# Low weights of feature pieces in the other half of a 256-byte stretch, and high and low products in turn

## What is computed

```
proj = rmsnorm(h) @ w_in                     # q, k, v, u, y of the first block
q = rmsnorm(h) @ w_cq; k, v = mem @ w_ck, mem @ w_cv
hid = square(relu(rmsnorm(h) @ w_mlp_in)); h = h + hid @ w_mlp_out
for l in range(2):
    z = rmsnorm(x) @ w_in[l]                 # all branches and 4 x 1024 gate logits
    for n in range(4): merged += sigmoid(gate[n]) * (o_branch[n] @ w_branch[l, n])
    x = x + merged @ w_out[l]
    g, u = split(rmsnorm(x) @ w_gate_up[l]); x = x + (silu(g) * u) @ w_down[l]
```

## Time and profile before

| | |
|---|---|
| median of 3 runs | 1287.14 us (1286.13 to 1290.83) |
| profiled execution | 1285.49 us |
| its span, first to last instruction | 1283.7 us |
| mean granted TensorE clock | 0.997 of full speed |
| PE busy | 1253.3 us (98%), 9,208 products |
| DVE busy | 862.3 us (67%) |
| ACT busy | 652.8 us (51%) |
| HBM read | 209.29 MB, 164 GB/s over the span |

### The profile page before, as it was taken

The page is one execution under the profiler, slowest core; times in us unless marked ns, Lnnn a source line. Parts: engine busy times, 40 slices in busy tenths (PEclk is TensorE's granted clock), DMA queues, the critical chain, the costliest instruction groups (busy, mean ns, idle before and its releaser), DMA issues.

```text
span 1283.7 us, 22072 instructions
## 1 busy us (share of the span) xinstructions
PE 1253.3 (98%) x9208; PEld 1171.8 (91%) x9208; DVE 862.3 (67%) x1194; ACT 652.8 (51%) x1049; POOL 116.8 (9%) x152
## 2 busy tenths in 40 slices
PE   8999999999999999998999999999999999999998
PEld 7998999988898889997999998888899988999987
DVE  6897677654457675998656554567577996655553
ACT  5896665543368553342544443566552434544432
POOL 2100100000000001661000000000003810000000
PEclk9999999999999999999999999999999999999999
DMA  9543445555533323442555555434333325455552
GB/s 370 207 164 120 177 138 194 195 197 197 197 116 148 132 101 130 165 164 86 180 195 183 181 195 197 164 132 150 109 137 132 134 97 198 164 185 179 195 197 99
DMA packets 30324, 211.77 MB, mean 165 GB/s; under 512 B 3344, under 2 KB 3728, under 8 KB 5264
## 3 DMA queue, kind: packets, MB, share of 16 engines
q1 hardware_dynamic: 29936, 210.22, 45.9%
q10 hardware_dynamic: 288, 0.14, 0.0%
HBM read 209.29 MB, written 1.05 MB: 164 GB/s over the span
## 4 chain that ended last, share of the span: by engine, by line
PE 73%; DVE 14%; ACT 6%; issue 5%; DMA 1%; DVEq 0%; ACTq 0%
PE bank L510 71%; DVE w_lo L1627 3%; ACT w_hi L1127 2%; DVE W L1601 2%; ACT W L1127 1%; PE bank L610 1%; PE bank L845 1%; DVE xs L2127 1%; DVE W L1587 1%; DVE W L2107 1%; DVE junk L2125 1%; DMA ring<-weight_pieces 1%; DVE W L1588 1%; DVE W L1619 1%; DVE stat L1560 0%
## 5 line engine op out<-in xcount | busy, mean ns | idle before, releaser
L1627 DVE TENSOR_TENSOR w_lo<-ring,w_hi 128x2048 fp32r<-128x2048 f32 x183 | 422.6, 2309 | 278.4 <-ACT w_hi L1127 278.1
L1127 ACT ACTIVATE w_hi<-ring 128x1024 fp32r<-128x1024 f32 (+1 forms) x368 | 366.2, 1046 | 234.5 <-PE bank L510 218.4
L510 PE MATMUL bank<-x_hi,w_hi 128*128 128x256 f32 x1840 | 264.5, 282 | 2.7 <-ACT w_hi L1127 2.7
L510 PE MATMUL bank<-x_hi,w_lo 128*128 128x256 f32 x1840 | 259.5, 279 | 1.4 <-DVE w_lo L1627 0.8
L510 PE MATMUL bank<-x_lo,w_hi 128*128 128x256 f32 x1840 | 252.5, 279 | 0.0
L510 PEld LDWEIGHTS bank<-x_hi,w_hi 128*128 128x128 f32 x1840 | 234.8, 188 | 6.3 <-issue 2.2
L510 PEld LDWEIGHTS bank<-x_hi,w_lo 128*128 128x128 f32 x1840 | 234.4, 188 | 2.8 <-DVE w_lo L1627 1.6
L510 PEld LDWEIGHTS bank<-x_lo,w_hi 128*128 128x128 f32 x1840 | 231.6, 188 | 0.0
L510 PE MATMUL bank<-W 128*128 128x128 f32 (+4 forms) x716 | 110.7, 327 | 8.5 <-ACT W L1127 4.9
L510 PEld LDWEIGHTS bank<-W 128*128 128x128 f32 (+3 forms) x716 | 87.7, 187 | 21.7 <-issue 12.5
L1106 POOL MEMSET W<- 128x512 f32 x32 | 16.9, 527 | 661.6 <-PE bank L510 658.4
(11 more groups left out here) (257 smaller groups left out, 1237.0 us busy)
## 6 DMA issues: line engine op xcount, KB each, us to landing
ring<-weight_pieces SPq DMA_DIRECT2D x191, 1024.0 KB, 4.8
const<-constants SPq DMA_DIRECT2D x1, 1376.5 KB, 10.3
W<-x_features SPq DMA_DIRECT2D x4, 256.0 KB, 5.3
ring<-weight_pieces SPq DMA_DIRECT2D x2, 512.0 KB, 6.2
h<-x SPq DMA_DIRECT2D x2, 512.0 KB, 11.8
W<-rg_weights SPq DMA_DIRECT2D x1, 1024.0 KB, 10.1
xs<-mem_features SPq DMA_DIRECT2D x1, 1024.0 KB, 10.7
oT<-mem SPq DMA_DIRECT2D x1, 1024.0 KB, 12.2
```

The source lines that it names most:

```text
L510: return nc.tensor.matmul(out, lhsT, rhs, start=first, stop=last)
L1127: return nc.scalar.activation(out, in_, ACT.Copy, scale=scale)
L1627: v.tensor_tensor(w_lo[:, q % SPLITS, 0:n], raw(pp)[:, 0:n], w_hi[:, q % SPLITS, 0:n].bitcast(F32), ALU.subtract).then_inc(s_weight_low, 1)
```

## The change

Each slot of `w_lo` becomes 32 floats (128 bytes) longer. A function `low_weights(q)` says where in its slot the low part of piece q lies: in token pieces at a multiple of 64 floats from where it lay before, in feature pieces 32 floats off that (in slot 0 by the offset c0 = 32, in slot 1 because the slot itself starts 32 later). `split` keeps the form of each piece. DVE writes there, and all users read there.

In the first half of a feature gemm without `parts`, PE waits for w_lo at the start; then for each k the product of the high weights and x_hi is followed by that of the low weights and x_hi; the eight products of the high weights and x_lo come last. The second half keeps its three passes.

```
-        w_lo = sb("w_lo", [P, SPLITS, PIECE], F32R)
+        w_lo = sb("w_lo", [P, SPLITS, PIECE + BANK], F32R)          # BANK = 32
...
+        def low_weights(q):
+
+            _, n, form = split[q]
+            c0 = BANK * (q % SPLITS ^ (form == "feat"))
+            return w_lo[:, q % SPLITS, c0:c0 + n]
...
-                hi, lo = (w[:, q % SPLITS, 0:KT * n].rearrange("p (k c) -> p k c", k=KT) for w in (w_hi, w_lo))
+                hi, lo = (w.rearrange("p (k c) -> p k c", k=KT) for w in (w_hi[:, q % SPLITS, :], low_weights(q)))
                 pe.wait_ge(s_weight_high, 2 * q + 1)
...
+                    if half == 0 and form == "feat":
+                        wait_low(pe, q)
+                        for k in range(KT):
+                            if k == KT // 2:
+                                pe.wait_ge(s_weight_high, 2 * (q + 1))
+                            product(0, k, hi, x_hi, k == 0, False)
+                            product(0, k, lo, x_hi, False, False)
+                        for k in range(KT):
+                            product(0, k, hi, x_lo, False, k == KT - 1)
+                        continue
                     for i, (w, x) in enumerate(passes):
...
-                    v.tensor_tensor(w_lo[:, q % SPLITS, 0:n], raw(pp)[:, 0:n], w_hi[:, q % SPLITS, 0:n].bitcast(F32), ALU.subtract).then_inc(s_weight_low, 1)
+                    v.tensor_tensor(low_weights(q), raw(pp)[:, 0:n], w_hi[:, q % SPLITS, 0:n].bitcast(F32), ALU.subtract).then_inc(s_weight_low, 1)
```

More of the change, by code:

```diff
@@ L47 @@
 SPLITS = 2
+BANK = 32
+FEATURE = ("u", "y", "q", "k", "ck", "cq", "a", "f", "e", "up", "gu", "gate")
 RG_C = 8.0
@@ L307, in build, with piece @@
         split_of = {}
-        def piece(n=PIECE):
+        def piece(n=PIECE, form=None):
             nonlocal pieces
@@ L313, in piece @@
                 split_of[pieces] = len(split)
-                split.append((pieces, n))
+                split.append((pieces, n, form if pieces else None))
             pieces += 1
@@ L320, in proj @@
         def proj(name, l=None, js=range(2), n=PIECE):
-            return [("proj", name, l, j, piece(n)) for j in js]
+            return [("proj", name, l, j, piece(n, "feat" if name in FEATURE else "tok")) for j in js]
+        def low_weights(q):
+            _, n, form = split[q]
+            c0 = BANK * (q % SPLITS ^ (form == "feat"))
+            return w_lo[:, q % SPLITS, c0:c0 + n]
         def wait_low(eng, q):
@@ L400, in build @@
             b, c, e, (hg,) = proj("b", l), proj("c", l), proj("e", l), proj("hg", l, (0,))
-            gates = [("gate", l, g, half, piece()) for g in range(4) for half in range(2)]
+            gates = [("gate", l, g, half, piece(form="feat")) for g in range(4) for half in range(2)]
             steps += [a[0], ("high", f0[-1]), ("low", f0[-1]), ("layerstat", l), a[1], f0, ("finalscale", l)]
@@ L414, in build @@
             steps += pairs("query", 1)
-            gates = [("gate", l, g, half, piece()) for g in range(4, 8) for half in range(2)]
+            gates = [("gate", l, g, half, piece(form="feat")) for g in range(4, 8) for half in range(2)]
             for i in range(len(LEVELS) + 1):
@@ L516, in first_gemm @@
                 bank = fill(job, "g")
-                hi, lo = (w[:, 0, :].rearrange("p (k c) -> p k c", k=KT) for w in (w_hi, w_lo))
+                hi, lo = (w[:, 0, 0:PIECE].rearrange("p (k c) -> p k c", k=KT) for w in (w_hi, w_lo))
                 for half, kh in ((0, 0), (0, 1), (1, None)):
@@ L714, in _ @@
                         q = split_of[p]
-                        hi, lo = (w[:, q % SPLITS, :].rearrange("p (k c) -> p k c", k=4) for w in (w_hi, w_lo))
+                        hi, lo = (w.rearrange("p (k c) -> p k c", k=4) for w in (w_hi[:, q % SPLITS, :], low_weights(q)))
                         pe.wait_ge(s_weight_high, 2 * (q + 1))
@@ L733, in _ @@
                         q = split_of[p]
+                        hi, lo = w_hi[:, q % SPLITS, :], low_weights(q)
                         bank = fill(job, "g")
@@ L736, in _ @@
                         wait_low(pe, q)
-                        for i, (w, x) in enumerate(((w_hi, x_hi), (w_hi, x_lo), (w_lo, x_hi))):
+                        for i, (w, x) in enumerate(((hi, x_hi), (hi, x_lo), (lo, x_hi))):
                             for k in range(KT):
-                                ins = mm(bank[:, 0:S], w[:, q % SPLITS, 32 * k:32 * k + P], x[:, k, :], i == k == 0, i == 2 and k == KT - 1)
+                                ins = mm(bank[:, 0:S], w[:, 32 * k:32 * k + P], x[:, k, :], i == k == 0, i == 2 and k == KT - 1)
                         full(ins, job)
@@ L754, in _ @@
                         q = split_of[p]
-                        hi, lo = (w[:, q % SPLITS, :].rearrange("p (k c) -> p k c", k=2) for w in (w_hi, w_lo))
+                        hi, lo = (w.rearrange("p (k c) -> p k c", k=2) for w in (w_hi[:, q % SPLITS, :], low_weights(q)))
                         if j == 0:
@@ L1137, in split_ahead @@
                 while done < min(split_of[p] + 1 + ahead, len(split)):
-                    q, (pp, n) = done, split[done]
+                    q, (pp, n, _) = done, split[done]
                     done += 1
```

## The result

The change makes the kernel slower by 0.6%: 1296.66 us (median of 4 runs, 1295.62 to 1297.02) against 1287.99 us for the kernel before beside it (4 runs, 1286.13 to 1290.83), a ratio of 1.0059 with a 95% interval of 1.0044 to 1.0074. That is +8.7 us; I had said +18.9. The profiled executions lie further apart than the medians: 1297.02 us (span 1295.2, mean clock 0.993) after, 1285.49 us before, which makes +11.5.

The account below looks back on a forecast made before the run. PE, busy in 98% of the span, was taken as the bound through its product pace and waits. Waits for w_lo summed to 21.6 us, pace change zero; on 1285.5 that makes 1307.1, stated as 1306 us (+1.5%), range 1290 to 1313.

Parts of the forecast that it names:

- The turns and the 128 bytes: Product pace on PE in feature gemms: gain up to 8.2 us effective, losses of 3.8 and 3.4; taken as zero.
- rival A: Nearly all feature gemms go to 113.3 ns, the gain eaten by waits: +8.7, or 1295 us; chance 0.28.
- `gu`: Every second piece stalls 0.36 us, eight a layer, plus pieces 3 and 4: 4.2 a layer, 8.5 for both.
- `up`: Pieces 5, 1 and 2 start late for w_lo: 1.4 plus 0.4, 1.8 us.
- The waits: PE's wait for w_lo moved ahead of product 1 of feature gemms without parts: 21.6 us in all, bounds 14 and 24.
- Gates 9 to 14: DVE sets the time, so PE moves back once, not six times: +2.0 a layer, 4.0 for both.
- `e`, gates 4 and 5 and `f` 0: Single late w_lo in both layers: 2.4 (of 3.5, bounds 0 and 3.5), 1.5 and 0.8 us.
- `u`, `y`, `ck` 1: Single late w_lo: 2.2 us for the first two together, 0.4 for the last.
- over 40 times and some 15 to 20 us: Sign in the waits view: how often and how long PE waits for w_lo, not 1.8 us as before.
- Rival B: The turns cost pace in feature gemms and the `up` stage: +29, or +25 with one loss, 1311 to 1315; chance 0.11.
- C: Most of the faster outcome, below the range given, with a pace below 113 ns; chance 0.09.
- Rival D: Late w_lo does not matter since DVE and ACT catch up, pace stays: +2 to +6, 1290; 0.12 including mixtures.

Follow-up runs that it names:

- the shift alone: Kernel before with only the low weights of feature pieces 128 bytes further, old passes and late wait: 1278.96 us against 1288.15, ratio 0.9921.
- the early wait alone: Kernel before with one edit, PE waits for w_lo ahead of the first product in feature gemms without parts: 1307.58 us, ratio 1.0143.
- with 256 bytes: Kernel before with only the low weights of feature pieces moved, by 256 bytes instead of 128: 1289.14 us, ratio 1.0000.
- the turns and no shift: Changed kernel's turns and wait for w_lo at the start, but low weights left where they lay before: 1305.93 us, ratio 1.0143.
- the shift with the wait: Changed kernel without its turns: low weights 128 bytes further, waited for ahead of the first product, old pass order: 1300.65 us against 1290.04, ratio 1.0082.

## Why the prediction was wrong, point by point

**The step that failed** is in "The turns and the 128 bytes": "I take zero". Its own bounds reached from 19.4 us of gain in all, 8.2 of it effective, to a loss, and the reason for zero was that after the turns 24 of 32 products have "the old meeting of addresses". That reads the pace as a property of the two addresses that meet. The runs show a state that PE keeps: the step from one place of the loaded weights to one 128 bytes on changes it, and the old place then holds it just as well (gate 4 of the shift alone, and the 21 other gemms there that become quick at their first low-weight pass). The prediction had half of this, "falls into one pace after a gap and keeps it", and in the rows of `f` 1 to `b` 0 it saw the pace change without a gap, where a new operand is loaded. It didn't draw the line from there to the low weights, which now lie in another place than the high ones, so that PE steps from one to the other at least twice in every gemm. The evidence against rival A, that w_lo and w_hi in their old places mostly fall to 117.8, said nothing on a step between places.

**What took its place** is the rival's working. The shift alone is worth -9.2 us, inside the changed kernel 19.4 - 8.7 = 10.7. Each difference is uncertain by 3.4 us or so, so the measured share of the shift could be some us off. Rival A came to +8.7 as measured. To the tenth that is luck, since between the two profiled executions it is +11.5 and a base uncertain by 1.6 was named; but its parts stand in the table:

- `gu`: 2.0 a layer said; 0.63 + 1.32 = 1.95 and 0.97 + 1.31 = 2.28 measured.
- `up`: 1.8 said, 1.85 measured.
- Gates: 3.8 said; 2.08 - 0.11 and 2.09 - 0.13, together 3.9.
- All else: 7.3 of waits less 8.2 of pace, -0.9 said; 2.29 - 0.88 - 0.16 = +1.25 measured.

**The waits** (21.6 us, bounds 14 and 24) are priced by the early wait alone: +19.4. Term by term, from the table:

- `gu`: 3.22 for eight pairs and, ahead of piece 3, 0.77 and 1.14: 4.0 and 4.4 a layer, 4.2 said. A pair pays 0.40 and not 0.36, every second piece, as worked out. Piece 4, which was to cost 0.58, doesn't wait in the trace of the early wait.
- Gates 9 to 14: 2.1 a layer, 2.0 said, and once: gate 8 to gate 9 takes 2.1 longer, and from gate 9 to gate 15 nothing is added but 0.2 in one layer. The reading that DVE sets the time there, and not six stalls, held.
- `up`: 2.3, 1.8 said. Part of it is pace: behind piece 0 PE goes on at 117.8 ns for four pieces.
- `e`, gates 4 and 5 and `f` 0: 4.7 said. From `a` 0 to gate 8 it is -0.6 and +0.7: absorbed, as far as a stretch shows it that differs by over a microsecond between kernels without a new wait. In layer 0 one sees where: PE's wait for ACT's xs, 1.9 us before, is 0.4 us with the early wait alone. I had taken 2.4 of 3.5 for `e` alone; zero was the bound that came true.
- `u`, `y`, `ck` 1: 2.6 said. The first stretch is 4.5 longer, but some 2 of that are not the wait's: it also takes 167.40 with the shift alone, 168.13 and 166.19 in the kernels with x_lo moved and 167.55 with 256 bytes. 165.64 is the quickest of all traces.

**How often PE waits** was said as "over 40 times and some 15 to 20 us". It is 30 times and 17.5 us. I counted some late pieces that no longer were, which ones stays open; the sum fits in part since with quicker gemms each w_lo in `gu` is later (idle 0.39 instead of 0.18). The other signs: the products of `gu` take 276 to 278 ns (279 before), near rival A's 276, and DVE is busy for 44.95 of 45.00 us between 529 and 574, so it doesn't wait for PE in the gates of layer 0.

**Rival B** failed: in the changed kernel the `up` stage kept its pace but for its first pieces, and the 120 ns show in single gemms (`f` 1). Only with the turns and no shift did `up` go at 117.8 ns, and kernels without turns do that too. For **C**, the outcome that has 0.09 of the chances and most of "Faster", no run shows a ground: a pace clearly below 113 ns came nowhere, and the best is 90.00 / 797 = 112.9 ns, in `gu` of the shift alone (113.0 before, in `up`). **Rival D** failed as a whole: w_lo in `gu` depends on the previous gemm's end, and the stall comes back each pair. Its mechanism held between `a` 0 and gate 8.

**What the runs leave open.** 128 bytes in the place of the loaded weights alone change the time by -0.8% (ratio 0.9921), with the order, the waits and all other engines' work left as they were. Whether PE meets another engine there or only itself, they don't show. Why 128 bytes do it, 64 at a price and 256 not, and why a shift of the loaded operand counts and one of the streamed does not, no run here settles.

## What to carry to other kernels

Where all products are bound by their spacing on TensorE, read that spacing as time over count in windows, and look for a second level of it: here two levels lie 4% apart, and 128 bytes in the place of one loaded operand moved most products to the quicker, at 256 bytes of SBUF a partition. An order of products that needs an operand earlier pays for producers that were hidden behind the old order (here +19.4 us for the early wait alone), so make the change of order in the part where the operand is there already, and ask whether it is needed: with the turns in the second half none of the stalls comes (0.9915), but the shift without any turns gets the same (0.9921). And price the parts of an edit apart, since a gain of 9 us and a loss of 19 looked here like one change that does little.

## What the runs showed that I had not expected

**Two spacings, and a way between.** 256-column products go at 113.3 or 117.8 ns for whole stages. With all weights in one kind of place either can come (what decides, no run shows): `up` at 113 and `gu` at 117 before, `up` at 117 and `gu` of layer 1 at 113 in the kernel with both weights shifted. The step of 128 bytes moved PE into the quick one and the step back didn't move it out; after a stall it could be lost (694.68 above). The token products lost some of it: 554 of their gaps are quick after, 769 before, 215 x 4.45 ns = 1 us.

**Behind a wait the clock can fall.** After the new wait ahead of gate 9 the granted clock falls. The timeline of PE there:

```profile
530.52 1.95 PE L518 MATMUL bank<-W 128*128 128x128 f32 x16
534.47 0.36 PE L518 MATMUL bank<-x_hi,w_hi 128*128 128x256 f32 x1 [2.01 <-DVE w_lo L1646]
...
535.59 0.41 PE L518 MATMUL bank<-x_hi,w_hi 128*128 128x256 f32 x1
535.80 0.41 PE L518 MATMUL bank<-x_hi,w_lo 128*128 128x256 f32 x1
536.02 0.41 PE L518 MATMUL bank<-x_hi,w_hi 128*128 128x256 f32 x1
```

All engines by window (PE, PEld, DVE, ACT, POOL, then the clock), at gate 9 and behind it:

```profile
533.00:541.00 8.00, 6.53 (x42) 6.56 (x43) 8.00 (x11) 3.68 (x5) 6.68 (x7) 0.79 0.37 132
541.00:549.00 8.00, 8.00 (x73) 8.00 (x72) 7.95 (x11) 3.68 (x5) 6.54 (x7) 1.00 0.38 131
```

After 2.01 us without a product and some 0.9 us of products at 117 ns, 16 follow each other at 213 ns; 16 x (213 - 113) ns is some 1.6 us. The granted clock is 0.50 from 535.50 to 537.20, where these products run, and 1.00 before the wait (530.00 to 532.50). It happens in both layers (a mean clock of 0.66 from 1002 to 1007, where the products are slow at once, 213 ns from 1003.00 on). The wait alone doesn't decide it: with waits of 1.8 to 2.1 us there in all four kernels that have the early wait, the clock falls in both layers of two (the changed one, and the turns without shift, with 0.66 from 540 to 545 and from 1010 to 1015), in layer 1 only of the early wait alone (0.73 from 1010 to 1015), and in neither of the shift with the wait (1.00 from 533 to 541 and from 1003 to 1011). It also falls in the kernel before, which has no such wait for w_lo: 0.72 from 433 to 439 and from 873 to 879, behind waits for ACT of 1.89 and 2.47 us. It costs nothing here, since DVE is busy for all 8.00 us of that window and gate 9 to gate 15 takes 51.38 us, 51.49 before. On a path of PE's own 1.6 us would come on top of the wait's 2.1, an estimate from these rows.
